# The first input tile's products with the high part of its weights, spread over the transposition stage

## The chip, the cores and the metric

The kernel runs on one core of one Trainium2 chip. The metric is the device time of one execution in microseconds. The engines are named PE (TensorE), ACT (ScalarE), DVE (VectorE), POOL (GpSimd) and SP (SyncE, which only starts DMAs here).

## The reference

One encoder block on 272 tokens (16 meta tokens and 256 of `x`) of width 2048, followed by an expert FFN. The change touches only the first norm and the first 128 columns of the projection behind it:

```python
def rms_norm(x, g):
    xf = x.astype(jnp.float32)
    y = xf * lax.rsqrt(jnp.mean(xf * xf, axis=-1, keepdims=True) + NORM_EPS)
    return (y * g.astype(jnp.float32)).astype(x.dtype)
...
    meta = jnp.broadcast_to(meta_tokens.astype(x.dtype)[None], (bsz, N_META, D_MODEL))
    hs = jnp.concatenate([meta, x], axis=1)
...
        h = rms_norm(hs, norm_mix[l])
        z = h @ w_in[l]
        u_ssm, q, k, v, gates = jnp.split(z, splits, axis=-1)
        y_a = s5_mixer(u_ssm, ssm_lam_re[l], ssm_lam_im[l], ssm_log_dt[l], ssm_b_re[l], ssm_b_im[l],
                       ssm_c_re[l], ssm_c_im[l], ssm_d[l], ssm_w_glu[l], ssm_b_glu[l])
...
        merged = g[:, :, 0] * (y_a @ w_proj_ssm[l]) + g[:, :, 1] * (y_b @ w_proj_attn[l])
        hs = hs + merged @ w_out[l]
        hs = hs + peer_ffn(rms_norm(hs, norm_ffn[l]), peer_w_q[l], peer_k1[l], peer_k2[l],
                           peer_u[l], peer_v[l])
```

## The kernel before

Each engine has its own program in program order; semaphores tie them. A counter such as `s_wdone` (tiles that PE has finished), `s_high` and `s_low` (high and low parts of weight tiles that are ready), `s_hT` and `s_hL` (blocks of the normed input that are ready) is waited on by value. Several counters are raised ahead of time so that the first buffers are free at once: `s_hT` and `s_hL` by 4, `s_uk` by 2.

**Transposition stage.** The rows of `xs` are the tokens, already divided by their root mean square. PE needs them with the 2048 channels on partitions, so for each of KT = 16 blocks of 128 channels it makes three transpositions into bank k % 4 of PSUM: one of the 16 meta tokens (L1372) and two of 128 tokens (L1374). ACT takes the bank, scales it by the norm's weight and rounds it to the high part `hH[k]` (L514); DVE takes the same bank once more and stores what the rounding left, `hL[k]` (L924). A step k of PE waits until `hH[k-4]` and `hL[k-4]` are there, that is, until its bank is free.

**Weight tiles.** A tile of weights, 128 x 2048, comes by DMA into one of the four slots of `ring`, from SP (L366). Its slot is free when PE has finished the tile four before it. ACT rounds it to the high part (`high`, L492), and DVE subtracts to get the low part (`low`, L826). For tile 0 POOL does the subtraction (L419), since DVE is busy with the norm. ACT's high part of tile 0 stands ahead of its sixteen `hH`; that of tile 1 stands right behind them, and DVE's low part of tile 1 right behind the sixteen `hL`. Both queues are strict.

**Column tiles.** For m = 0 to 9 (W_V = 10) PE makes `split_product` into bank m % 2: for each block k the high weights with `hH[k]` (L1359), the same weights with `hL[k]` (L1360) and the low weights with `hH[k]` (L1361), 48 products of 272 columns. Tile 0 waits for the last `hL` and for POOL's low part (`s_first`); each later tile waits for its own low part (`s_low`) and for a bank that ACT has read (`s_uk`). ACT reads a finished tile (L534) behind the high part of the tile two further on, which the same finished tile releases. POOL, meanwhile, copies `hH` and `hL` once the last `hL` is there (L424, L425).

Beside the column tiles DVE works on the coefficients of the state-space part between its low parts. Behind them come value tiles (the first use of banks 2 to 4 after the transpositions), queries and attention, the scan with the gate products, the projections and the expert FFN.

Of the kernel before, what the change touches and what calls it, by code (L numbers as in the profile page):

```python
# [20 lines left out]
ACT = mybir.ActivationFunctionType  # L21
AX_X = mybir.AxisListType.X

P = 128
D = 2048
KT = D // P
META, SEQ = 16, 256
L = META + SEQ
# [18 lines left out]
W_UK, W_V, W_Q, W_GATE, W_GLU, W_PROJ, W_OUT, W_PQ, W_END = 0, 10, 12, 20, 52, 56, 72, 88, 104  # L47
# [11 lines left out]
H2 = L // 2  # L59
# [7 lines left out]
def build(nc, W, keys, par, bw, cw, meta, x, gffn, gfin, u_tab, v_tab, out):  # L67
    top = ExitStack()
    with top:
        def sem(name):  # L70
            return top.enter_context(nc.semaphore(name))

        def sbt(stack, name, shape, dt=F32):
            return stack.enter_context(nc.sbuf_tensor(name, shape, dt))
# [28 lines left out]
        hH = sbt(mix, "hH", [P, KT, L], F32R)  # L103
        yaL, = over(("yaL", [P, CT, SEQ]))
        ukT = sbt(mix, "ukT", [P, 10, L])
# [21 lines left out]
        hL = sbt(pre, "hL", [P, KT, L], F32R)  # L127
# [76 lines left out]
        ps = top.enter_context(nc.psum_tensor("ps", [P, 8, 512], F32))  # L204
# [13 lines left out]
        def wlow(n, m, c):  # L218

            return low_ring[:, n % RING, :].rearrange("p (m c) -> p m c", m=m, c=c)  # L220

        def high_slot(n):

            return (wh1 if n < W_GATE else wh2 if n < W_OUT or n % 4 < 2 else wh3)[:, n % 2, :]

        def whigh(n, m, c):
            return high_slot(n).rearrange("p (m c) -> p m c", m=m, c=c)
# [9 lines left out]
        def nth_low(n):  # L237
            return n - 1 if n < W_Q else W_Q - 1 + n - W_PROJ
# [7 lines left out]
        s_wdone = sem("s_wdone")  # L246
        s_high, s_low = sem("s_high"), sem("s_low")
        s_first = sem("s_first")
# [5 lines left out]
        s_hT, s_hL = sem("s_hT"), sem("s_hL")  # L254
# [52 lines left out]
        s_fsq, s_frt, s_fin, s_out = (sem(n) for n in ("s_fsq", "s_frt", "s_fin", "s_out"))  # L307

        LAG = 2
        FIRST_HALVES = ((), ((2, 0), (2, 1)), ((3, 0),), ((3, 1),), ((4, 0),), ((4, 1),), ((5, 0),), ((5, 1),))  # L310
        FIRST_MINUS = (((2, 0), (2, 1)), ((3, 0), (3, 1)), ((4, 0),), ((4, 1),), ((5, 0),), ((5, 1),), (), ((6, 0), (6, 1)))
        FIRST_OUT = ((0,), (1,), (2,), (), (3,), (), (4,), ())
# [8 lines left out]
        def behind(b, t, k):  # L321

            return (b, t - k) if t >= k else (b - 1, t - k + PPL)
# [152 lines left out]
        def _(act):  # L476
# [10 lines left out]
            def high(n, i=0, back=2):  # L487

                act.wait_ge(s_w[n % RING], 16 * (nth_load(n) + 1) + 16 * i)
                if back:  # L490
                    act.wait_ge(s_wdone, RING + n - back + 1 + RING * i)
                nc.scalar.activation(high_slot(n), ring[:, n % RING, :], ACT.Copy).then_inc(s_high, 1)  # L492
# [29 lines left out]
            for m in range(W_V):  # L522
                act.wait_ge(s_wdone, RING + m + 1)
                high(m + 2)
                if m == SINES:

                    act.wait_ge(s_f0, 1)
                    nc.scalar.activation(disc[:, 6, :], disc[:, 4, :], ACT.Sin, scale=TWO_PI).then_inc(s_trig0, 1)
                    nc.scalar.activation(disc[:, 7, :], disc[:, 4, :], ACT.Sin, scale=TWO_PI / 2).then_inc(s_trig0, 1)
                if m < CT:  # L530
                    for j in range(4):
                        for q in range(2):
                            at = 64 * (j % 2) + 32 * q
                            ins = nc.scalar.activation(ukT[at:at + 32, m, H2 * (j // 2):H2 * (j // 2 + 1)], ps[32 * j:32 * j + 32, m % 2, q:L:2], ACT.Copy)  # L534
                else:
                    ins = nc.scalar.activation(ukT[:, m, :], ps[:, m % 2, 0:L], ACT.Copy)
                ins.then_inc(s_uk, 1)
# [69 lines left out]
            def minus_high(b, t, half):  # L607
                use, q = gate_half(b, t, half)
                act.wait_ge(s_gc[q], 16 * use + 16)
                nc.scalar.activation(gate_lo(q), gate_hi(q), ACT.Copy, scale=-1.0).then_inc(s_gn, 1)  # L610

            def take_y(b, cc):

                ct = 2 * b + cc
                act.wait_ge(s_y, PPC * ct + PPC + PPL)
                for j in range(4):
                    for q in range(2):
                        at = 64 * (j % 2) + 32 * q
                        ins = nc.scalar.activation(flat(yT[32 * j:32 * j + 32, bass.ds(ct, 1), q::2]),
                                                   ps[at:at + 32, 6 + cc, KEPT * (j // 2) + q:KEPT * (j // 2) + q + SEQ // 2], ACT.Copy)  # L620
                ins.then_inc(s_ye, 1)
# [12 lines left out]
            def gate(b, t):  # L634

                g = SPC * b + t
                act.wait_ge(s_wdone, RING + W_GATE + 1 + g)
                nc.scalar.activation(flat(gates_v[:, bass.ds(g, 1), :]), ps[:, t % 2, 0:SEQ], ACT.Identity,  # L638
                                     bias=prm[:, bass.ds(COLS["bgate"][0] + g, 1)]).then_inc(s_gs, 1)

            def scan_body(b, first=False, last=False):
                for t in range(PPL):
# [17 lines left out]
                    else:  # L660
                        gate(*behind(b, t, LAG + 1))
                    if t == PPL - 1:
# [10 lines left out]
            minus_high(*behind(BODIES, 0, 1), 1)  # L673
            gate(*behind(BODIES, 0, LAG + 1))
            act.wait_ge(s_ye, 2 + CT - 1)
            nc.scalar.activation(yT[:, 0:CT - 1, :], yT[:, 0:CT - 1, :], ACT.Gelu_apprx_tanh).then_inc(s_gel, 1)
            gate(*behind(BODIES, 1, LAG + 1))
            take_y(BODIES - 1, 1)
            act.wait_ge(s_ye, 2 + CT)
            nc.scalar.activation(yT[:, CT - 1, :], yT[:, CT - 1, :], ACT.Gelu_apprx_tanh).then_inc(s_gel, 1)  # L680
            gate(*behind(BODIES, LAG, LAG + 1))
            nc.scalar.activation(ybH[:, :, :], ybT[:, :, :], ACT.Copy).then_inc(s_ybh, 1)
# [651 lines left out]
        def _(pe):  # L1334
# [20 lines left out]
            def split_product(dst, n0, xh, xl, ks=range(KT), block0=0, last=KT - 1):  # L1355

                wh, wl = whigh(n0, KT, P), wlow(n0, KT, P)
                for k in ks:
                    nc.tensor.matmul(dst, wh[:, block0 + k, :], xh(k), start=(k == 0), stop=False)  # L1359
                    nc.tensor.matmul(dst, wh[:, block0 + k, :], xl(k), start=False, stop=False)  # L1360
                    ins = nc.tensor.matmul(dst, wl[:, block0 + k, :], xh(k), start=False, stop=(k == last))  # L1361
                return ins


            pe.wait_ge(s_par, 16)
            pe.wait_ge(s_xs, TT)
            pe.wait_ge(s_xsm, 1)
            for k in range(KT):
# [4 lines left out]
                for t in range(TT):  # L1373
                    ins = nc.tensor.transpose(ps[:, k % 4, META + t * P:META + (t + 1) * P], xs[:, t, c], ident)  # L1374
                ins.then_inc(s_tr, 1)
            pe.wait_ge(s_hL, 4 + KT)

            for m in range(W_V):
                if m == 0:
                    pe.wait_ge(s_first, 1)  # L1380
                else:
                    pe.wait_ge(s_low, nth_low(m) + 1)
                pe.wait_ge(s_uk, m + 1)
                split_product(ps[:, m % 2, 0:L], m, lambda k: hH[:, k, :], lambda k: hL[:, k, :]).then_inc(s_wdone, 1)

            for k in range(KT):
# [4 lines left out]
                for t in range(TT + 1):  # L1391
# [5 lines left out]
                    ins = nc.tensor.matmul(dst, hH[:, k, c], wl, start=False, stop=(k == KT - 1))  # L1397
# [60 lines left out]
            def half_gate(b, t, half):  # L1458
                use, q = gate_half(b, t, half)
                if half == 0:  # L1460
                    pe.wait_ge(s_gs, SPC * b + t + 1)
                half_tile(t, half, HEADS // RING + SPC // RING * b + t // RING, q, use)
# [112 lines left out]
            def scan_body(b, first=False, last=False):  # L1575
                for t in range(PPL):
                    cc = t // PPC
                    if first:
                        for g, half in FIRST_HALVES[t][0:1]:
                            half_gate(b, g, half)  # L1580
                    else:
                        half_gate(*behind(b, t, LAG), 0)
                    if t % PPC == 3:
# [11 lines left out]
                    if first:  # L1595
                        for g, half in FIRST_HALVES[t][1:]:
                            half_gate(b, g, half)
                    else:
                        half_gate(*behind(b, t, LAG), 1)

# [46 lines left out]
            for c in range(4):  # L1647
                pe.wait_ge(s_hs, 2 * c + 2)
                for g in range(4):
# [5 lines left out]
                    for k in range(4 * g, 4 * g + 4):  # L1655
                        for T in range(TT):
# [3 lines left out]
                            ins = nc.tensor.matmul(dst, mH[:, k, rows], wl[:, k % 4, :], start=False, stop=(k == KT - 1))  # L1660
# [35 lines left out]
            for T in range(TT):  # L1696
                tokens = slice(T * P, (T + 1) * P)
                for q in range(2):
                    weights_in(W_PQ + q)
                    w = wtile(W_PQ + q, KT, P)  # L1700
                    for k in range(KT):
                        if T == 0 and q == 0 and k == KT - 4:
                            pe.wait_ge(s_h2T, 4 + KT)
                        ins = nc.tensor.matmul(ps[:, 4 + q, tokens], w[:, k, :], h2T[:, k, tokens], start=(k == 0), stop=(k == KT - 1))
                    ins.then_inc(*((s_fp, 1) if T == 0 else (s_wdone, 1)))
                pe.wait_ge(s_key, 16)
                for half in range(2):
                    pe.wait_ge(*((s_fq, half + 1) if T == 0 else (s_qp, 3 + half)))
                    ins = nc.tensor.matmul(ps[:, 6, (2 * T + half) * NK:(2 * T + half + 1) * NK], qp[:, half, tokens],
                                           keyt[:, 0, half, :], start=True, stop=True)  # L1710
# [112 lines left out]
```

## Time and profile before

| what | us |
|---|---|
| median of 3 runs | 2058.37 |
| lowest, highest | 2055.93, 2059.32 |
| the profiled execution | 2053.23 |
| its span, first to last instruction | 2051.4 |
| PE busy in it | 1748.9 |

The span is the time from the first to the last instruction of the profiled execution; its device time is 1.8 us longer. All times of the trace are counted from the span's start. A timeline row has the start, the busy time, the engine, the line, the operation, output and inputs, their shapes, the number of instructions merged in the row, and in brackets the idle time ahead of it and who ended it. A PE row's busy time reaches to the end of its pipeline, so the distance between the starts of two rows, not their busy time, is what a product costs in a dense row of them.

### The profile page before, as it was taken

How to read it: one execution, taken by the hardware profiler on the slowest of the kernel's cores; microseconds unless marked ns; L12 is line 12 of the kernel's file. 1: busy time of each engine (PE TensorE's matmuls, PEld its weight loads, DVE VectorE, ACT ScalarE, POOL GpSimd, SP SyncE). 2: the span in 40 equal slices, each digit the busy share in tenths (PEclk: the TensorE clock that was granted, in tenths of full speed). 3: DMA queues.
4: the chain of work that ended last, by engine and by line, in shares of the span. 5: the costliest groups of instructions: out<-in, count | busy, mean ns of one | idle time of the engine just before them, and what ended most of it. 6: DMA issues, size and time to landing. Idle time of an engine off the chain costs nothing.

```text
span 2051.4 us, 23984 instructions
## 1 busy us (share of the span) xinstructions
PE 1748.9 (85%) x7792; PEld 1091.3 (53%) x7792; DVE 1286.3 (63%) x2444; ACT 475.7 (23%) x1056; POOL 805.0 (39%) x711
## 2 busy tenths in 40 slices
PE   6999899999999999789879977777777777778776
PEld 5988788888998855335425522233232222223222
DVE  4635888885454455665667667667666665666654
ACT  6533555655343201101011001002000000000001
POOL 2022233330540053454445554444554554554431
PEclk9999999999999999999999999999999999999999
DMA  4578789987455699999999999999999999999997
GB/s 186 164 173 184 173 193 209 213 193 237 168 187 182 223 394 421 421 421 422 422 422 422 418 422 421 421 422 413 421 418 411 422 417 389 422 404 412 422 422 298
DMA packets 115890, 687.60 MB, mean 335 GB/s; under 512 B 12880, under 2 KB 12880, under 8 KB 41168
## 3 DMA queue, kind: packets, MB, share of 16 engines
q0 software_dynamic: 96768, 589.34, 75.7%
q1 hardware_dynamic: 19040, 97.24, 13.4%
q8 instruction: 42, 0.69, 0.1%
q14 instruction: 40, 0.33, 0.0%
HBM read 684.44 MB, written 2.10 MB: 335 GB/s over the span
## 4 chain that ended last, share of the span: by engine, by line
PE 46%; DMA 35%; issue 7%; DVE 6%; POOL 4%; ACT 1%; DVEq 0%; POOLq 0%; SPq 0%; ACTq 0%
DMA uv<-u_tab,eid 31%; PE ps L1726 14%; PE ps L1442 4%; PE ps L1676 3%; PE ps L1359 2%; PE ps L1360 2%; PE ps L1361 2%; POOL uv L472 2%; DMA parts<-W 2%; PE ps L1447 2%; DVE uv L1295 2%; PE ps L1449 2%; PE ps L1448 2%; PE ps L1659 1%; PE ps L1658 1%
## 5 line engine op out<-in xcount | busy, mean ns | idle before, releaser
L1726 PE MATMUL ps<-uv,dg 128*128 128x512 f32 x2048 | 959.6, 615 | 265.6 <-DVE dg L1301 256.6
L1295 DVE CUSTOM_DVE_ANT_0 uv<-uv,xn 128x2048 f32<-128x2048 f32 x256 | 586.9, 2293 | 377.4 <-DMA uv<-u_tab,eid 359.1
L1726 PEld LDWEIGHTS ps<-uv,dg 128*128 128x128 f32 x2048 | 381.1, 194 | 821.7 <-issue 458.8
L472 POOL DMA_INDIRECT uv<-v_tab,eid x256 | 274.9, 1074 | 590.9 <-PE ps L1726 360.4
L469 POOL DMA_INDIRECT uv<-u_tab,eid x256 | 353.0, 1379 | 199.5 <-issue 184.9
L772 ACT ACTIVATE ga<-av 128x1 f32<-128x1 f32 x256 | 51.9, 203 | 1185.1 <-DVE av L1295 1185.1
L826 DVE TENSOR_TENSOR low_ring<-ring,wh 128x2048 fp32r<-128x2048 f32 x43 | 101.0, 2352 | 76.6 <-ACT wh L492 76.6
L1301 DVE TENSOR_SCALAR dg<-prm,ga,gw 128x128 f32<-128x128 f32 x256 | 95.0, 371 | 66.8 <-ACT ga L772 32.6
L1447 PE MATMUL ps<-hH,parts 128*128 128x256 f32 x400 | 123.8, 310 | 2.4 <-DMA parts<-W 2.3
L442 POOL DMA_DIRECT2D parts<-W x80 | 70.4, 880 | 139.3 <-ACT parts L610 111.7
L438 POOL DMA_DIRECT2D parts<-W x80 | 47.1, 588 | 179.6 <-PE ps L1449 111.9
L1449 PE MATMUL ps<-hH,parts 128*128 128x256 f32 x400 | 112.2, 280 | 0.0
L1448 PE MATMUL ps<-hLx,parts 128*128 128x256 f32 x400 | 112.2, 280 | 0.0
L1442 PE MATMUL ps<-xn,ring 128*128 128x256 f32 x480 | 111.6, 382 | 0.1
L492 ACT ACTIVATE wh<-ring 128x2048 fp32r<-128x2048 f32 x44 | 84.3, 1917 | 114.7 <-PE ps L1361 82.1
L1676 PE MATMUL ps<-h2T,ring 128*128 128x256 f32 x448 | 100.8, 379 | 0.0
L1676 PEld LDWEIGHTS ps<-h2T,ring 128*128 128x128 f32 x448 | 85.0, 190 | 21.8 <-issue 11.5
L1442 PEld LDWEIGHTS ps<-xn,ring 128*128 128x128 f32 x480 | 88.3, 190 | 12.7 <-ACT gates L638 0.7
L1447 PEld LDWEIGHTS ps<-hH,parts 128*128 128x128 f32 x400 | 75.3, 188 | 8.7 <-issue 4.7
L1448 PEld LDWEIGHTS ps<-hLx,parts 128*128 128x128 f32 x400 | 75.6, 189 | 1.0
L1449 PEld LDWEIGHTS ps<-hH,parts 128*128 128x128 f32 x400 | 75.4, 188 | 0.0
L610 ACT ACTIVATE parts<-parts 128x640 fp32r<-128x640 f32 x60 | 44.0, 734 | 94.5 <-DMA parts<-W 94.5
(284 smaller groups left out, 2238.3 us busy)
## 6 DMA issues: line engine op xcount, KB each, us to landing
ring<-W SPq DMA_DIRECT2D x64, 1024.0 KB, 4.8
parts<-W POOLq DMA_DIRECT2D x160, 320.0 KB, 5.4
ring<-W SPq DMA_DIRECT2D x40, 384.0 KB, 5.2
xn<-x SPq DMA_DIRECT2D x4, 1024.0 KB, 8.2
uv<-u_tab,eid POOLq DMA_INDIRECT x256, 15.5
uv<-v_tab,eid POOLq DMA_INDIRECT x256, 14.2
bwt<-bw SPq DMA_DIRECT2D x8, 256.0 KB, 6.0
cwt<-cw SPq DMA_DIRECT2D x8, 256.0 KB, 6.1
```

Source lines behind the costliest of these rows:

```text
L469: pool.indirect_dma_start(uv[:, s, 0, :], None, u_tab, at).then_inc(s_u[s], 16)
L472: pool.indirect_dma_start(uv[:, s, 1, :], None, v_tab, at).then_inc(s_vv[s], 16)
L492: nc.scalar.activation(high_slot(n), ring[:, n % RING, :], ACT.Copy).then_inc(s_high, 1)
L826: nc.vector.tensor_tensor(low_ring[:, n % RING, :], ring[:, n % RING, :], high_slot(n), ALU.subtract).then_inc(s_low, 1)
L1295: nc.vector.tensor_tensor_reduce(uv[:, j % UV, 0, :], uv[:, j % UV, 0, :], xn[:, T, :], 1.0, 0.0, ALU.mult, ALU.add, av[:, hh, j:j + 1]).t ...
L1301: nc.vector.tensor_scalar(dg[:, j % 2, :], ident, ga[:, hh, j:j + 1], gw[:, hh, j:j + 1], ALU.mult, ALU.mult).then_inc(s_dg, 1)
L1442: nc.tensor.matmul(dst, whole(t)[:, k, :], hX[:, k, :], start=(k == 0), stop=False)
L1447: nc.tensor.matmul(dst, wh[:, m, :], hH[:, k, META:L], start=False, stop=False)
L1448: nc.tensor.matmul(dst, wh[:, m, :], hLx[:, k, :], start=False, stop=False)
L1449: ins = nc.tensor.matmul(dst, wl[:, m, :], hH[:, k, META:L], start=False, stop=(k == 2 * PART - 1))
L1676: ins = nc.tensor.matmul(ps[:, 4 + q % 2, 0:SEQ], w[:, k, :], h2T[:, k, :], start=(k == 0), stop=(k == KT - 1))
L1726: ins = nc.tensor.matmul(ps[:, 4 * T + n, :], dg[:, j % 2, :], uv[:, j % UV, 1, n * 512:(n + 1) * 512], start=False, stop=last and i == 2 ...
```

## The change

The column tile 0 is taken out of the loop over tiles. It gets bank 4 (`FIRST_BANK`) in place of bank 0, which the transpositions use. From step k = 4 on, PE makes two products of tile 0, high weights with `hH[k-4]` and with `hL[k-4]`, behind the transpositions of step k. The pairs 12 to 15 come after the last transpositions, each behind a wait for its `hL`. Then come the 16 products with the low weights, now in one row, and `s_wdone` is raised as before. ACT reads tile 0 from bank 4. Nothing changes on the queues of DVE, POOL and SP.

```diff
+        FIRST_BANK = 4
...
-                            ins = nc.scalar.activation(ukT[at:at + 32, m, H2 * (j // 2):H2 * (j // 2 + 1)], ps[32 * j:32 * j + 32, m % 2, q:L:2], ACT.Copy)
+                            ins = nc.scalar.activation(ukT[at:at + 32, m, H2 * (j // 2):H2 * (j // 2 + 1)], ps[32 * j:32 * j + 32, m % 2 if m else FIRST_BANK, q:L:2], ACT.Copy)
...
             pe.wait_ge(s_par, 16)
+            wh0, wl0 = whigh(0, KT, P), wlow(0, KT, P)
+            first_out = ps[:, FIRST_BANK, 0:L]
+
+            def high_terms(k):
+                nc.tensor.matmul(first_out, wh0[:, k, :], hH[:, k, :], start=(k == 0), stop=False)
+                nc.tensor.matmul(first_out, wh0[:, k, :], hL[:, k, :], start=False, stop=False)
+
             pe.wait_ge(s_xs, TT)
             pe.wait_ge(s_xsm, 1)
             for k in range(KT):
...
                 ins.then_inc(s_tr, 1)
-            pe.wait_ge(s_hL, 4 + KT)
-
-            for m in range(W_V):
-                if m == 0:
-                    pe.wait_ge(s_first, 1)
-                else:
-                    pe.wait_ge(s_low, nth_low(m) + 1)
+                if k >= 4:
+                    pe.wait_ge(s_high, 1)
+                    high_terms(k - 4)
+            for k in range(KT - 4, KT):
+                pe.wait_ge(s_hL, 4 + k + 1)
+                high_terms(k)
+            pe.wait_ge(s_first, 1)
+            for k in range(KT):
+                ins = nc.tensor.matmul(first_out, wl0[:, k, :], hH[:, k, :], start=False, stop=(k == KT - 1))
+            ins.then_inc(s_wdone, 1)
+
+            for m in range(1, W_V):
+                pe.wait_ge(s_low, nth_low(m) + 1)
                 pe.wait_ge(s_uk, m + 1)
                 split_product(ps[:, m % 2, 0:L], m, lambda k: hH[:, k, :], lambda k: hL[:, k, :]).then_inc(s_wdone, 1)
```

PE's instructions at the steps 3 to 5 of the transposition stage, before (`prm` holds the identity matrix, `gates` is the memory of `xs`):

```order
7 L1372 MATMUL ps<-prm,gates 128x16
8 L1374 MATMUL ps<-prm,gates 128x128 x2
9 L1372 MATMUL ps<-prm,gates 128x16
10 L1374 MATMUL ps<-prm,gates 128x128 x2
11 L1372 MATMUL ps<-prm,gates 128x16
12 L1374 MATMUL ps<-prm,gates 128x128 x2
```

The same place of PE's queue in the changed kernel, where L1380 and L1382 are the transpositions and L1371 and L1372 the pair of `high_terms`:

```order
7 L1380 MATMUL ps<-prm,gates 128x16
8 L1382 MATMUL ps<-prm,gates 128x128 x2
9 L1380 MATMUL ps<-prm,gates 128x16
10 L1382 MATMUL ps<-prm,gates 128x128 x2
11 L1371 MATMUL ps<-hH,wh 128x272
12 L1372 MATMUL ps<-hL,wh 128x272
13 L1380 MATMUL ps<-prm,gates 128x16
14 L1382 MATMUL ps<-prm,gates 128x128 x2
15 L1371 MATMUL ps<-hH,wh 128x272
16 L1372 MATMUL ps<-hL,wh 128x272
```

Two products of tile 0 now stand between the transpositions of one step and those of the next, from step 4 on.

PE's instructions from the last transpositions into tile 0, before:

```order
31 L1372 MATMUL ps<-prm,gates 128x16
32 L1374 MATMUL ps<-prm,gates 128x128 x2
33 L1359 MATMUL ps<-hH,wh 128x272
34 L1360 MATMUL ps<-hL,wh 128x272
35 L1361 MATMUL ps<-hH,low_ring 128x272
36 L1359 MATMUL ps<-hH,wh 128x272
```

And in the changed kernel, from the last transpositions to the first products of tile 1 (L1360 to L1362 are `split_product` there):

```order
53 L1380 MATMUL ps<-prm,gates 128x16
54 L1382 MATMUL ps<-prm,gates 128x128 x2
55 L1371 MATMUL ps<-hH,wh 128x272
56 L1372 MATMUL ps<-hL,wh 128x272
57 L1371 MATMUL ps<-hH,wh 128x272
58 L1372 MATMUL ps<-hL,wh 128x272
...
63 L1371 MATMUL ps<-hH,wh 128x272
64 L1372 MATMUL ps<-hL,wh 128x272
65 L1392 MATMUL ps<-hH,low_ring 128x272 x16
66 L1360 MATMUL ps<-hH,wh 128x272
```

Between the last transpositions and tile 1 there are five pairs and the sixteen low-part products, 26 products in place of 48.

## Rows read from the trace of the kernel before

**Rows 1.** Busy time of each engine by stretches of 10 us, columns named.

```profile
core 0: us, PE busy (x) PEld busy (x) DVE busy (x) ACT busy (x) POOL busy (x), PEclk, DMA share, GB/s
20.00:30.00 10.00, 8.89 (x33) 5.26 (x32) 5.50 (x11) 6.54 (x12) 1.32 (x2) 1.00 0.00 0
40.00:50.00 10.00, 10.00 (x83) 10.00 (x82) 5.88 (x14) 5.91 (x14) 0.00 (x0) 1.00 0.47 160
```

**Rows 2.** Timeline of the transposition stage; last row: L1374 alone, duration ns min/median/max, starts.

```profile
13.79 1.89 ACT L492 ACTIVATE wh<-ring 128x2048 fp32r<-128x2048 f32 x1
...
14.45 0.26 PE L1372 MATMUL ps<-prm,gates 16*128 16x16 f32 x1 [14.45 <-DVE gates L919]
...
15.25 0.28 PE L1372 MATMUL ps<-prm,gates 16*128 16x16 f32 x1
...
26.09 0.28 PE L1372 MATMUL ps<-prm,gates 16*128 16x16 f32 x1
...
26.30 0.69 PE L1374 MATMUL ps<-prm,gates 128*128 128x128 f32 x2
...
26.92 0.28 PE L1372 MATMUL ps<-prm,gates 16*128 16x16 f32 x1
27.03 0.49 ACT L514 ACTIVATE hH<-ps,prm 128x272 fp32r<-128x272 f32 x1 [0.35 <-PE ps L1374]
...
27.55 0.50 DVE L924 SCALAR_TENSOR_TENSOR hL<-ps,prm,hH 128x272 fp32r<-128x272 f32 x1 [0.34 <-ACT hH L514]
...
L1374 PE MATMUL ps<-prm,gates x32: 420/448/476, 14.6 to 27.4; 128*128 128x128 f32 x32
```

**Rows 3.** Timeline, from the last hH to the middle of tile 0.

```profile
27.86 0.49 ACT L514 ACTIVATE hH<-ps,prm 128x272 fp32r<-128x272 f32 x1 [0.35 <-PE ps L1374]
28.24 1.90 ACT L492 ACTIVATE wh<-ring 128x2048 fp32r<-128x2048 f32 x1
...
28.93 0.59 PE L1359 MATMUL ps<-hH,wh 128*128 128x272 f32 x1 [1.11 <-DVE hL L924]
28.96 3.49 POOL L424 TENSOR_TENSOR xn<-hH,hL 128x1536 f32<-128x1536 f32 x1 [8.68 <-DVE hL L924]
...
29.33 0.43 PE L1360 MATMUL ps<-hL,wh 128*128 128x272 f32 x1
...
30.18 4.42 DVE L826 TENSOR_TENSOR low_ring<-ring,wh 128x2048 fp32r<-128x2048 f32 x1 [1.30 <-ACT wh L492]
...
32.27 0.41 PE L1361 MATMUL ps<-hH,low_ring 128*128 128x272 f32 x1
...
32.50 0.31 PE L1359 MATMUL ps<-hH,wh 128*128 128x272 f32 x1
```

**Rows 4.** Timeline of PE, SP and DVE where tile 1 follows tile 0.

```profile
36.51 0.28 PE L1361 MATMUL ps<-hH,low_ring 128*128 128x272 f32 x1
36.63 0.29 PE L1359 MATMUL ps<-hH,wh 128*128 128x272 f32 x1
...
36.97 6.30 SPq L366 DMA_DIRECT2D ring<-W  x2
...
38.87 2.29 DVE L826 TENSOR_TENSOR low_ring<-ring,wh 128x2048 fp32r<-128x2048 f32 x1 [4.27 <-ACT wh L492]
```

**Rows 5.** Timeline of PE, then stretches (columns as rows 1), scan stage.

```profile
218.72 0.39 PE L1447 MATMUL ps<-hH,parts 128*128 128x256 f32 x1 [2.31 <-DMA parts<-W]
...
251.76 1.97 PE L1484 MATMUL ps<-prm,hs 128*128 128x128 f32 x8
...
220.30:223.60 3.30, 3.30 (x50) 2.89 (x49) 3.30 (x9) 0.00 (x0) 1.43 (x2) 0.50 0.70 147
251.00:254.30 3.30, 3.30 (x24) 2.85 (x23) 3.22 (x10) 0.00 (x0) 0.00 (x0) 0.50 1.05 264
254.40:257.80 3.40, 3.40 (x23) 2.92 (x20) 3.21 (x9) 3.38 (x9) 0.87 (x1) 1.00 0.69 174
```

**Rows 6.** Waits from 0 to 130 us: who waited for whom, total, times, longest.

```profile
POOL parts L438 <- PE ps L1361: 54.9, 1, 54.9
```

## The prediction

> **What bounds the kernel now.** The change touches only the first 40 us, so I read that stretch. The view by stretches first: from 40 us on PE is busy 10.00 us of 10 while the ten column tiles of the first projection run, but from 20 to 30 us only 8.89 [rows 1]. So whatever moves the start of the first PE-bound tile moves everything behind it, and the question is what sets that start.
>
> The timeline of one step of the transposition stage comes next [rows 2]. Step k is one 16-column product at L1372 and two 128-column ones at L1374, then ACT's hH[k], then DVE's hL[k]. The L1372 rows stand at 26.09 and 26.92, a pitch of 0.83 us, and sixteen steps fill 14.45 to 27.8, when the last hH starts [rows 3]. Is it PE or ACT that sets this pitch? ACT works 0.49 us of each 0.83 and is idle for 0.34 of it, released by PE L1374; DVE works 0.50 and waits for ACT. Nobody is full but PE, whose matmul rows leave no hole. Nor can it be ACT's release that paces PE: a step waits for step k-4 alone, done over two microseconds earlier, and steps 0 and 1, which wait for no hH at all, already stand 0.80 us apart (14.45 and 15.25) [rows 2]. **The transposition stage is PE-bound**, and this is what the change loads further.
>
> Then the end of the stage [rows 3]. The last hH runs at 27.86, ACT makes the high part of tile 1 at 28.24 (1.90 us), DVE its low part at 30.18 for 4.42 us, ready at 34.60. PE starts tile 0 at 28.93 after 1.11 us of idleness. Its products stand 0.226 us apart up to 32.27 (272 columns in 0.226 us is the 1.2 GHz level) and 0.125 us apart from 32.50 on (33 of them up to 36.63), the 2.4 GHz level. (The granted-clock column reads 1.00 before that, because its record starts there; the spacing of the rows is what I go by.) Tile 1 starts at 36.63, straight behind tile 0 [rows 4]. So there are two chains to tile 1: PE's own, which ends at 36.6, and hH[15] - high(1) - low(1), which ends at 34.6. The second has only 2.0 us of slack.
>
> **The change, part by part.** Nothing is computed less: 32 of tile 0's 48 products go elsewhere. 22 of them (11 pairs, after the steps 4 to 14) now stand ahead of the transpositions of step 15, one more pair behind step 15, four pairs behind that, then 16 low-part products.
>
> What it can gain: PE's idle 1.11 us, and less behind the stage. But even with PE's chain at nothing, tile 1 can't start before 34.60, its low part's end. The gain is capped at 36.63 - 34.60 = 2.0 us, 0.1% of the span.
>
> What it costs: each pair at the 1.2 GHz pace is 2 x 0.226 = 0.45 us in the middle of a stage that PE bounds. From below, a pair could take 0.32 us, if it also fills the 0.13 us by which the last product of a step is longer than such a transposition back to back. That last one: the two L1374 end at 26.30 + 0.69 = 26.99, one alone takes 0.42, so the second began at 26.57, 0.35 us ahead of the next L1372 [rows 2]. Back to back it is (1.97 - 0.42) / 7 = 0.22 us: eight L1484 took 1.97 at the low level [rows 5]. From above 0.62 us: the first product behind the stage took 0.40 us to the next (28.93 to 29.33 [rows 3]) and one more at 0.226. I take 0.45, since satisfied waits cost nothing at a tile change (36.51 to 36.63 is the plain spacing [rows 4]), and the added waits on s_high are satisfied from 15.7 on (13.79 + 1.89 us, ACT's first high part [rows 2]). That delays hH[15] by 11 x 0.45 = 5.0 us (3.5 to 6.8), and with it, on unchanged ACT and DVE queues, high(1) and low(1). Low(1) takes 4.42 us where the next one takes 2.29 [rows 3, 4]; what differs is POOL's copying beside it (L424 from 28.96, L425 behind it). That waits for the last hL, so it moves along and low(1) stays long. Ready: 34.60 + 5.0 = 39.6.
>
> PE's chain meanwhile: step 15's transpositions end at about 32.8, high pair 11 at 33.2, pairs 12 to 14 by 34.6, pair 15 by 35.0 (its hL is ready just ahead of 28.93 + 5.0 = 33.9). The 16 low-part products end between 37.0 (16 x 0.125) and 38.6 (16 x 0.226). At either clock **PE then waits 1.0 to 2.6 us for low(1)**, and tile 1 starts at about 39.65 instead of 36.63: **+3.0 us**, with the bounds of the pair +1.5 to +4.8.
>
> Edits costed at nothing, and their cover: the other bank (ACT's eight reads of tile 0 are the same reads from another bank, and bank 4 is next written by the value tiles, eight tiles later); the load of tile 4, which waits for tile 0's end, 36.97 before [rows 4] and at most 38.6 now, 6.3 us for two, wanted only four tiles on, at some 6.0 us each (11 us of cover or more); high(2), released by tile 0's end as well, wanted when tile 1 ends, six us later. Does a later stage take the 3 us back? DVE's low parts are released by ACT's high parts and those by PE's tile counter; POOL's weight streams wait 54.9 us for that counter [rows 6]. Each is released by PE's progress, so all shift together, and I carry the whole +3.0 us to the end.
>
> **What the clock may do.** The rows show two things that disagree. The transposition stage ran from 14.45 to 27.8 us, and the products behind it still started at the low level's spacing [rows 2, 3]. But later, from 251.0 to 254.3, at granted clock 0.50, PE ran eight transpositions L1484 without a gap, with a few products ahead of them and behind, and went up straight after (0.50, then 1.00) [rows 5]. The difference that I see is density: eight transpositions in 1.97 us there, three in 0.83 us with pauses here.
>
> The Trainium skill ("TensorE: Matmul & The Clock Gate", Part 4: PE-mode transpose) says that the full clock doesn't engage for transposes, since they don't count as busy time in the same way. By that rule only the pairs would count in the new mixture, and the sum stands as it is; the stage before agrees with it, the rows from 251 us on are hard to square with it. Were transpositions to count in full, the sum would be that of rival 1.
>
> **The rivals.** Rival 1, the clock rises within the mixed stretch. For it: the rows at 251 us, and a denser PE. Against: 13.4 us of transpositions that didn't do it; pairs are only 0.45 of 1.28 us. Price: if it rises at about 23 us, four pairs have cost 1.8 us, and each remaining step of 0.83 shrinks to some 0.55 (an estimate: its products at half the time, its pauses unchanged) while its pair costs 0.25, so these break even. hH[15] is some 1.6 us late, low(1) ready at 36.2: tile 1 at 36.3, -0.4 us. The earliest rise gives the cap, -2.0. So 2058.0, still no measurable change.
>
> Rival 2, on the other side: **the new hole drops the clock or keeps it low, and tile 1 starts at 1.2 GHz.** Before, PE ran without a hole from 28.93, and was at the high level 3.6 us later. Now 1.0 to 2.6 us of idleness stand ahead of tile 1. An idle 2.31 us before 218.72 was followed by granted clock 0.50 at 220.3 [rows 5]. 3.6 us at the low level do the work of 2.0, so 1.6 us more: +4.6 us, 2063.0. It decides where the hole is 2 us or so, or where the clock hasn't risen by 39.6.
>
> Rival 3, the loss is hidden: some later wait (the DMA waits at 113 to 220 us) isn't released by PE and absorbs the 3 us: 2058.4. Against: the release chain told above.
>
> **How the numbers follow.** The profiled execution spans 2051.4 us and took 2053.2; the median of the runs is 2058.4 (2055.9 to 2059.3). I add to the median: 2058.4 + 3.0 = **2061.4 us**. Chances: forecast 0.45, rival 2 0.25, rival 1 0.20, rival 3 0.10. Range: down to 2057.0, which takes in most of rival 1 and 3; up to 2064.6, which takes in rival 2 and the forecast with a pair at 0.62 us (+4.8). A measurement of this kernel can tell about 0.2%, 4.1 us, from no change. Slower by more than that: three quarters of rival 2, and the upper fifth of the forecast: 0.28. Faster by that is beyond the cap of 2.0 us, and only scatter gives it: 0.03. Within 0.2%: 0.69.
>
> **What the new profile would show.** Pitch of L1380 (the old L1372): 0.83 for the first four steps, then 1.28. Last hH at 32.8 instead of 27.86; DVE's low part of tile 1 from 35.2 to 39.6, and PE idle before tile 1, released by DVE low_ring. If the pitch falls to 0.8 or less in the middle, rival 1 holds; if the first products of tile 1 stand 0.226 us apart, rival 2. A pair that costs much less than 0.45 us, or a tile 1 that doesn't wait for its low part, would break the sum. If tile 1 starts near 39.6 but the span is as before, it is rival 3.

## The result, and the profile after

| | us, median | lowest to highest | runs |
|---|---|---|---|
| before | 2055.61 | 2052.48 to 2061.20 | 22 |
| after | 2059.86 | 2054.51 to 2063.12 | 22 |

The ratio is 1.0016, with a 95% interval of 1.0011 to 1.0022: the changed kernel takes 3.3 us more (2.3 to 4.5). The two medians alone lie 4.25 us apart. The loss is real, and by the ratio it is within the 0.2% (4.1 us) that the prediction set as the bound of "no change"; by the medians it lies just at that bound. The forecast was +3.0 us.

In the timeline of the changed kernel the stage reads as it was worked out. One step with a pair, rows of PE, ACT and DVE (columns as in rows 2):

```profile
20.28 0.57 PE L1371 MATMUL ps<-hH,wh 128*128 128x272 f32 x1
20.65 0.43 PE L1372 MATMUL ps<-hL,wh 128*128 128x272 f32 x1
20.66 0.49 ACT L515 ACTIVATE hH<-ps,prm 128x272 fp32r<-128x272 f32 x1 [0.80 <-PE ps L1382]
21.01 0.28 PE L1380 MATMUL ps<-prm,gates 16*128 16x16 f32 x1
21.18 0.50 DVE L925 SCALAR_TENSOR_TENSOR hL<-ps,prm,hH 128x272 fp32r<-128x272 f32 x1 [0.79 <-ACT hH L515]
21.23 0.69 PE L1382 MATMUL ps<-prm,gates 128*128 128x128 f32 x2
...
22.30 0.28 PE L1380 MATMUL ps<-prm,gates 16*128 16x16 f32 x1
```

The starts of L1380 are 1.29 us apart, where [rows 2] had 0.83 between the same instructions, then L1372: a pair costs 0.45 us. ACT's idle time ahead of each hH has grown from 0.35 to 0.80 us, by that same 0.45: PE still paces the stage, and ACT waits for it longer. PE is busy for 10.00 us of the stretch from 20 to 30 us, which was 8.89 in [rows 1]. The busier PE has gained nothing.

The end of the stage and the start of tile 1, the rows that answer to [rows 3, 4]:

```profile
32.24 0.49 ACT L515 ACTIVATE hH<-ps,prm 128x272 fp32r<-128x272 f32 x1 [0.80 <-PE ps L1382]
32.63 1.91 ACT L493 ACTIVATE wh<-ring 128x2048 fp32r<-128x2048 f32 x1
...
33.35 3.49 POOL L425 TENSOR_TENSOR xn<-hH,hL 128x1536 f32<-128x1536 f32 x1 [13.66 <-DVE hL L925]
...
34.27 2.55 PE L1392 MATMUL ps<-hH,low_ring 128*128 128x272 f32 x16
34.57 8.75 DVE L827 TENSOR_TENSOR low_ring<-ring,wh 128x2048 fp32r<-128x2048 f32 x2 [1.30 <-ACT wh L493]
...
39.04 0.39 PE L1360 MATMUL ps<-hH,wh 128*128 128x272 f32 x1 [2.22 <-DVE low_ring L827]
39.27 0.29 PE L1361 MATMUL ps<-hL,wh 128*128 128x272 f32 x1
39.40 0.29 PE L1362 MATMUL ps<-hH,low_ring 128*128 128x272 f32 x1
```

The last hH starts at 32.24 instead of 27.86, the low part of tile 1 at 34.57 instead of 30.18 (the row merges two low parts; the first ends at 39.0), and PE, which in the kernel before went on to tile 1 at 36.63 without a wait, is idle for 2.22 us until DVE's low part is there. Tile 1 starts at 39.04. This execution's stage began 0.6 us earlier (13.85, against 14.45 in [rows 2]), so from the first transposition tile 1 is 3.0 us later (25.19 against 22.18). The products of tile 1 stand 0.12 us apart: it runs at the 2.4 GHz level from the start.

The spans of the two profiled executions differ by more, 2060.1 against 2051.4 us. That isn't the change: the profiled execution of before, 2053.23 us, lies near the low end of that kernel's range, that of after, 2061.96, near the high end of its own. Of the 8.7 us only 3.1 lie between the first transposition and tile 2.

For the experiments I read one number of each trace besides the runs: from the first transposition to the first product of tile 2, by which the start of the kernel and the clock's later dips drop out. It is 28.16 us before and 31.27 after.

### The profile page after: what moved, and what is told of

Same layout as the page of the kernel before. It is cut to its first block, busy times and chain, and to the rows that moved or that the text cites. A ratio compares the mean times of both kernels' runs of the same rounds, so it can differ in the third digit from the quotient of the medians.

```text
span 2060.1 us, 23983 instructions
## 1 busy us (share of the span) xinstructions
PE 1756.0 (85%) x7792; PEld 1096.2 (53%) x7792; DVE 1287.8 (63%) x2444; ACT 476.1 (23%) x1056; POOL 795.7 (39%) x711
## 4 chain that ended last, share of the span: by engine, by line
PE 44%; DMA 35%; issue 8%; DVE 7%; POOL 4%; ACT 1%; DVEq 0%; POOLq 0%; ACTq 0%; SPq 0%
DMA uv<-u_tab,eid 31%; PE ps L1740 13%; PE ps L1456 4%; DMA parts<-W 3%; POOL uv L473 3%; PE ps L1690 3%; PE ps L1360 2%; PE ps L1361 2%; PE ps L1362 2%; DVE uv L1296 2%; PE ps L1461 2%; PE ps L1463 2%; PE ps L1462 2%; PE ps L1673 1%; PE ps L1672 1%
## 5 line engine op out<-in xcount | busy, mean ns | idle before, releaser
L470 POOL DMA_INDIRECT uv<-u_tab,eid x256 | 340.5, 1330 | 199.5 <-issue 184.0
```

Of the source, the lines that this page charges most:

```text
L470: pool.indirect_dma_start(uv[:, s, 0, :], None, u_tab, at).then_inc(s_u[s], 16)
```

## Experiments

Each was run in five rounds beside the kernel before. Ratios and gains in us are against that kernel, with 95% intervals in brackets.

**Pairs behind the stage.** From the changed kernel:

```diff
-                if k >= 4:
-                    pe.wait_ge(s_high, 1)
-                    high_terms(k - 4)
-            for k in range(KT - 4, KT):
+            pe.wait_ge(s_high, 1)
+            for k in range(KT):
                 pe.wait_ge(s_hL, 4 + k + 1)
                 high_terms(k)
```

> Bank 4 and the order pairs first, low products last are kept, but all 16 pairs stand behind the transpositions of step 15; nothing is interleaved. Theory (the loss is the pairs inside the PE-bound stage, which delay hH[15] and so the low part of tile 1): step pitch stays 0.83 us, hH[15] and the low part of tile 1 stand as in the kernel before, and PE only gains its 1.1 us of idleness ahead of tile 0: tile 1 starts 1 to 1.5 us earlier relative to the first transposition (34.6 is the floor), so -1 to -1.5 us. Rival (the loss comes from the other bank, or from the order of the 48 products with the low ones last): still +3 us.

Ratio 0.9987 (0.9978 to 0.9996), -2.7 us (-4.5 to -0.8). First transposition to tile 2: 26.86 us, 1.3 less than before. Timeline of PE and ACT at the end of the stage:

```profile
26.79 0.28 PE L1380 MATMUL ps<-prm,gates 16*128 16x16 f32 x1
26.90 0.49 ACT L515 ACTIVATE hH<-ps,prm 128x272 fp32r<-128x272 f32 x1 [0.35 <-PE ps L1382]
...
27.01 0.69 PE L1382 MATMUL ps<-prm,gates 128*128 128x128 f32 x2
...
27.35 0.57 PE L1371 MATMUL ps<-hH,wh 128*128 128x272 f32 x1
```

The products follow the last transposition without the 1.11 us of waiting in [rows 3], and ACT's 0.35 us is back. So neither the bank nor the order of the 48 products costs anything; what costs is where the eleven pairs stand. The forecast of -1 to -1.5 us lies within the interval, and the trace gives -1.3. The version is faster than both kernels; against the one before it is 0.13%.

**Six pairs in the stage instead of twelve** (five ahead of step 15):

```diff
-                if k >= 4:
+                if k >= 10:
                     pe.wait_ge(s_high, 1)
-                    high_terms(k - 4)
-            for k in range(KT - 4, KT):
+                    high_terms(k - 10)
+            for k in range(KT - 10, KT):
```

> Pairs only behind the steps 10 to 15, five of them ahead of the transpositions of step 15 instead of eleven; the other ten pairs behind the stage. Theory: hH[15] later by 5 x 0.45 = 2.3 us instead of 5.0; the low part of tile 1 is ready at 36.9 where it was 34.6, so tile 1 starts 0.3 us later than before: +0.3 us, no measurable change, and PE waits for the low part only some tenths of a us. Rival (any interleaving costs the same, by a switch of mode between transpositions and products): near +3 us.

Ratio 1.0000 (0.9991 to 1.0009); 28.77 us to tile 2, 0.6 more than before. The size is as forecast (+0.3 us, no measurable change), and a fixed cost of any interleaving, +3 us, is ruled out. But the trace got there by another way. Timeline of PE:

```profile
23.51 0.28 PE L1380 MATMUL ps<-prm,gates 16*128 16x16 f32 x1
...
24.80 0.28 PE L1380 MATMUL ps<-prm,gates 16*128 16x16 f32 x1
...
26.06 0.23 PE L1380 MATMUL ps<-prm,gates 16*128 16x16 f32 x1
...
26.84 0.23 PE L1380 MATMUL ps<-prm,gates 16*128 16x16 f32 x1
...
35.08 0.39 PE L1360 MATMUL ps<-hH,wh 128*128 128x272 f32 x1 [2.10 <-DVE low_ring L827]
...
36.58 0.43 PE L1361 MATMUL ps<-hL,wh 128*128 128x272 f32 x1
36.80 0.43 PE L1362 MATMUL ps<-hH,low_ring 128*128 128x272 f32 x1
```

Two full steps take 1.29 us; from 26.0 on they take 0.78: the clock rose in the mixed stage, which is rival 1. Tile 0 was finished early, PE stood idle for 2.10 us, and within tile 1 the spacing goes to 0.22 us: the clock fell, which is rival 2. The stretches show the granted clock (columns as rows 1):

```profile
36.30:39.60 3.30, 3.30 (x17) 3.30 (x16) 3.27 (x3) 0.85 (x4) 0.91 (x1) 0.50 0.28 117
39.70:42.60 2.90, 2.90 (x26) 2.90 (x25) 0.90 (x4) 0.00 (x0) 0.00 (x0) 1.00 0.00 0
```

Tile 1 took 7.61 us (35.08 to 42.69) where it takes 5.98 in [rows 4]'s kernel: 1.6 us, the price that the prediction gave for this.

**The second chain cut.** The high part of tile 1 is made behind hH[5], its low part on POOL behind that of tile 0; DVE's own `low(1)` goes, and PE waits for `s_first` at 2 ahead of tile 1:

```diff
                 nc.scalar.activation(hH[:, k, :], ps[:, k % 4, 0:L], ACT.Copy, scale=col("gmix", k, k + 1)).then_inc(s_hT, 1)
-            high(1)
+                if k == 5:
+                    high(1)
...
             pool.tensor_tensor(low_ring[:, 0, :], ring[:, 0, :], high_slot(0), ALU.subtract).then_inc(s_first, 1)
+            pool.wait_ge(s_high, 2)
+            pool.tensor_tensor(low_ring[:, 1, :], ring[:, 1, :], high_slot(1), ALU.subtract).then_inc(s_first, 1)
```

> The changed kernel with the second chain cut: ACT makes the high part of tile 1 behind hH[5] instead of behind hH[15], and POOL makes its low part behind that of tile 0. Theory: the step pitch stays 1.28 us, but tile 1 starts right behind tile 0, at 36.7 instead of 39.04 on the changed kernel's clock: 2.4 us of the 3 come back, so +0.6 to +0.9 us against the kernel before. Rival (the loss is PE's own work at the low clock, not the wait for the low part): stays at +3.

Ratio 0.9994 (0.9984 to 1.0003), -1.2 us (-3.3 to +0.6); 28.69 us to tile 2, +0.5. The step pitch is still 1.29 us. Timeline of PE, the last of tile 0 and the first of tile 1:

```profile
35.23 1.67 PE L1395 MATMUL ps<-hH,low_ring 128*128 128x272 f32 x12
36.74 0.29 PE L1363 MATMUL ps<-hH,wh 128*128 128x272 f32 x1
```

No bracket: tile 1 follows at once. With the pairs just as they are in the changed kernel, 2.6 of the 3.1 us are gone as soon as tile 1 doesn't hang on hH[15]. That shows the chain hH[15], high(1), low(1) to carry the loss. The forecast for the runs, +0.6 to +0.9 us, lies at or just beyond the upper end of what they gave; the trace's +0.5 is close to it.

**One low product more** in each of the steps 8 to 15 (`low_term(k - 8)` behind `high_terms(k - 4)`, the other eight behind the stage):

```diff
                     high_terms(k - 4)
+                if k >= 8:
+                    pe.wait_ge(s_first, 1)
+                    low_term(k - 8)
```

> The changed kernel with one low product of tile 0 more in each of the steps 8 to 15, so three products beside the transpositions; seven of them ahead of step 15. Theory: hH[15] later by another 7 x 0.226 = 1.6 us, tile 1 too: +4.6 us against the kernel before, step pitch 1.51 us in these steps. Rival 1 of the prediction (a denser PE raises the clock in the mixed stage): the pitch falls below 1.2 us in the last steps and the total is +1 to +3 us.

Ratio 1.0011 (1.0002 to 1.0021), +2.3 us (+0.4 to +4.3). The pitch is 1.51 us for five steps, as forecast, then the clock rises at 30.9 and the last step takes 0.90. So rival 1 came true here, late. It brought nothing: PE waited 4.2 us for the low part of tile 1, the clock was low from 37.8 to 44.5, and the profiled execution has tile 2 at 33.96 us. Timeline of PE at tile 1:

```profile
39.58 0.59 PE L1360 MATMUL ps<-hH,wh 128*128 128x272 f32 x1 [4.20 <-DVE low_ring L827]
```

That is 5.8 us later than in the kernel before, where the runs lose 2.3: this execution took the longest of its eleven (2062.08 us). That the clock went another way in the others is likely, but not shown. The run doesn't tell how the loss grows with the number of products moved, since the clock moved with it.

**POOL's copies later.** The changed kernel, with POOL waiting for DVE's low part of tile 1 before it copies:

```diff
             pool.wait_ge(s_hL, 4 + KT)
+            pool.wait_ge(s_low, 1)
```

> The changed kernel, in which POOL's two copies of hH and hL wait until DVE has made the low part of tile 1. If that low part takes 4.4 us because POOL copies beside it, it takes 2.3 us now and ends at 36.9 instead of 39.0; tile 1 starts there, 0.4 us behind tile 0's end, and 2.1 of the 3 us come back: about +0.9 us against the kernel before. The next low part then runs beside the copies, but has cover. If POOL is not the cause, it stays at 4.4 us and the total at +3.

Ratio 1.0005 (0.9996 to 1.0014), +1.0 us (-0.8 to +2.9); 29.15 us to tile 2, +1.0. Timeline of DVE, then of POOL:

```profile
34.71 2.29 DVE L828 TENSOR_TENSOR low_ring<-ring,wh 128x2048 fp32r<-128x2048 f32 x1 [1.30 <-ACT wh L494]
39.37 3.44 DVE L828 TENSOR_TENSOR low_ring<-ring,wh 128x2048 fp32r<-128x2048 f32 x1 [2.36 <-ACT wh L494]
```

```profile
37.14 3.52 POOL L426 TENSOR_TENSOR xn<-hH,hL 128x1536 f32<-128x1536 f32 x1 [17.30 <-DVE low_ring L828]
40.60 4.39 POOL L427 CAST hLx<-hL 128x2560 fp32r<-128x2560 f32 x1
```

The low part of tile 1 takes 2.29 us instead of 4.42, ends as tile 0 does, and in the trace two thirds of the loss are gone (2.1 of 3.1 us). The next low part now meets POOL's copy and shows how: it starts at 39.37 under L426, which ends at 40.66, and ends at 42.81, 2.15 us after. It looks as if it stood still until POOL was done and then ran at its own pace. [Rows 3] fit the same: L424 ends at 32.45, low(1) at 34.60, 2.15 us after. In the changed kernel the copy ends at 36.84 and low(1) at 38.99, again 2.15 us after. POOL waits in its turn. Timeline of POOL in the version where it makes low(1) itself and DVE's next low part starts only at 38.97:

```profile
36.97 2.34 POOL L428 CAST hLx<-hL 128x2560 fp32r<-128x2560 f32 x1
```

The same cast took 4.40 us in the changed kernel, where DVE's low part ran for its first 2.2 us. The Trainium skill ("SBUF — State Buffer", SBUF: two separate sides) says just this, that VectorE and GpSimd share a pair of ports as an exclusive lock and the later one is blocked for the whole instruction; the 2.15 us, the same each time, agree with it.

**A warm start.** A "warm start" means here that PE reaches the stage at the 2.4 GHz level. To price a pair at that level, PE makes products of a constant tile, whose result nobody reads, while it waits for the norm anyway. The first form, on the kernel before, has 40 of them; each runs as two instructions:

```diff
+            pe.wait_ge(s_warm, 1)
+            for _ in range(40):
+                nc.tensor.matmul(ps[:, 5, 0:256], ucur[:, 0, 0:128], ucur[:, 0, 0:256], start=True, stop=True)
```

> The kernel before with 40 products of 128x256 (a constant tile, result never read) on PE ahead of the transposition stage, where PE waits for the norm anyway; they begin at about 2 us. They take 0.43 us each at the low level and 0.23 at the high one, so the clock rises among them and the stage starts at the high level. If transpositions alone keep the clock up, the step pitch is some 0.55 us throughout, the stage is 3 to 4 us shorter and tile 0 runs at 0.125 us a product: -4 to -6 us. If they don't count, the pitch is short for some steps only, the clock falls within the stage, and the gain is 1 to 2 us at most, with tile 0 as before.

> The changed kernel with the same 40 products ahead. Tells whether the mixed stage can hold the high level where it could not reach it. Theory (the price of a pair is that of the low level): if the clock holds, a pair costs at most 0.25 us, the step pitch is below 0.85 us, and the changed kernel's loss of 3 us is gone: -3 to -6 us against the kernel before, about the same as the kernel before with the warm start. If the clock falls in the stage: pitch 1.28 again after some steps, 0 to +3 us.

> The version with all pairs behind the stage (-2.7 us measured) and the 40 products ahead. If the high level survives the stage or a part of it, this gains what the warm start gains on the kernel before plus up to 1.3 us: -4 to -7 us; if the clock falls within the stage, -2 to -4 us.

Kernel before with it: ratio 1.0014 (1.0005 to 1.0023), +2.9 us. Changed kernel: 1.0024 (1.0015 to 1.0033), +4.9 us. Pairs behind: 1.0009 (1.0000 to 1.0018), +1.9 us. The gains forecast for a clock that holds were 4 to 6, 3 to 6 and 4 to 7 us; in all three traces it held through the stage, and all three forecasts were misses. I had mis-sized the filling, which I took for 40 instructions: it lasts until 21.4 us and delays the stage by 7 us. The inside of the stage still answers the question. Stretches of the kernel before with the warm start, the filling and the stage (columns as rows 1):

```profile
6.40:21.00 14.60, 14.60 (x69) 12.84 (x68) 4.42 (x14) 7.95 (x8) 4.51 (x1) 1.00 0.91 378
21.40:30.00 8.60, 8.56 (x49) 5.36 (x48) 6.98 (x15) 7.32 (x16) 0.00 (x0) 1.00 0.00 0
```

and its timeline of PE, then two steps of the changed kernel with the same start:

```profile
21.41 0.23 PE L1377 MATMUL ps<-prm,gates 16*128 16x16 f32 x1
...
21.94 0.23 PE L1377 MATMUL ps<-prm,gates 16*128 16x16 f32 x1
```

```profile
27.51 0.23 PE L1385 MATMUL ps<-prm,gates 16*128 16x16 f32 x1
...
27.86 0.37 PE L1376 MATMUL ps<-hH,wh 128*128 128x272 f32 x1
28.07 0.29 PE L1377 MATMUL ps<-hL,wh 128*128 128x272 f32 x1
28.29 0.23 PE L1385 MATMUL ps<-prm,gates 16*128 16x16 f32 x1
```

There are sixteen bare steps at 0.53 us, the high level held for 8.6 us of nothing but transpositions; with a pair, a step takes 0.78. So a pair costs 0.45 us at the low level and 0.25 at the high one, and the change loses at either: in the traces it is 4.0 us behind the kernel before with the same start (25.75 against 21.73 us to tile 2). Of these, 2.4 us are tile 1's later start, ahead of which PE waits 3.18 us for the low part, and 1.6 the clock, which falls at 40.6. By the ratios it is 2 us.

**A shorter filling**, 20 in place of 40:

> The kernel before with 20 of the leading products instead of 40 (each runs as two instructions, so 40 of them in place of 80): they end at 12.7 to 13.9 us, before the stage needs PE. The version with 40 had the stage start at 21.4 in place of 14.4 and still lost only 2.9 us; its steps were 0.53 us apart and tile 2 began 21.7 us behind the first transposition, against 28.2. If the start of the stage stays at 14.4: -6.4 us. If the clock falls in the short hole before the stage or in it, -1 to -3 us.

> The changed kernel with 20 leading products. With 40 its steps were 0.78 us apart where they carry a pair and 0.53 where not, so a pair costs 0.25 us at the high level. Eleven pairs delay hH[15] by 2.75 us against the kernel before with the warm start, and the low part of tile 1 is what PE waits for (3.2 us of idleness with 40): tile 1 some 2.5 us later than in e8_warm20_before, and the hole may bring the clock down for tile 1, 1.6 us more: -2 to -4 us against the kernel before. So the change loses at the high level too.

> Pairs behind the stage with 20 leading products: as e8_warm20_before, but PE starts tile 0 1.1 us earlier; tile 1 is then bound by its low part, so 0 to -1 us beyond e8_warm20_before: -6 to -7 us.

> The same with the high part of tile 1 made behind hH[5] and its low part on POOL, so that tile 1 follows tile 0 without a hole: another 0 to 1.3 us, -6.5 to -8.5 us against the kernel before.

| kernel with 20 | ratio, 95% interval | us | first transposition at | to tile 2 |
|---|---|---|---|---|
| before | 0.9993 (0.9985 to 1.0002) | -1.4 | 13.98 | 26.83 |
| after | 1.0009 (1.0000 to 1.0019) | +1.9 | 14.07 | 28.51 |
| pairs behind | 0.9976 (0.9966 to 0.9986) | -4.9 | 14.18 | 21.72 |
| pairs behind, low(1) on POOL | 0.9982 (0.9973 to 0.9990) | -3.7 | 14.02 | 24.61 |

The filling now ends in time, but the high level doesn't always survive the stage: in the kernel before the steps were 0.53 us, then 0.83 from 17 us on. Stretches of it, filling, first steps, the rest:

```profile
6.90:12.90 6.00, 6.00 (x29) 5.13 (x27) 3.44 (x14) 5.07 (x7) 0.00 (x0) 1.00 1.01 421
14.00:17.10 3.10, 2.89 (x17) 1.85 (x18) 1.40 (x4) 2.85 (x6) 1.80 (x1) 1.00 1.02 423
17.20:25.00 7.80, 7.80 (x29) 4.20 (x28) 4.89 (x11) 4.64 (x10) 2.62 (x1) 0.50 0.29 119
```

In the version with the pairs behind it held throughout. The same stretch there:

```profile
14.10:22.80 8.70, 8.42 (x49) 5.46 (x50) 6.60 (x14) 8.03 (x16) 4.53 (x1) 1.00 0.62 256
```

Up to the last transposition PE's program is the same in these two kernels, so the difference in the clock is one between executions and not one of code. With it, tile 1 started at 29.81, and tile 2 stood 6.4 us earlier in its stage than in the kernel before.

The last version is another matter. Timeline of ACT and PE in it, then a stretch:

```profile
17.90 1.90 ACT L497 ACTIVATE wh<-ring 128x2048 fp32r<-128x2048 f32 x1
...
20.86 0.20 PE L1388 MATMUL ps<-prm,gates 16*128 16x16 f32 x1 [1.26 <-DVE hL L930]
...
21.00:25.00 4.00, 4.00 (x16) 2.19 (x15) 2.70 (x7) 2.26 (x5) 3.40 (x1) 0.50 0.01 4
```

ACT's high part of tile 1 stands here ahead of hH[6]. At steps of 0.53 us four banks don't cover its 1.90 us: PE is idle for 1.26 us ahead of step 10, and the rest of the stage runs at the low level. At the pitch of 1.29 us the same move of high(1) cost PE nothing. Whether this hole brought the clock down isn't shown, as it fell without one in the kernel before.

Of the four forecasts two were plain misses. The changed kernel was to gain 2 to 4 us and lost 1.9; in its trace the clock fell early in the stage, and once more behind a hole of 3.20 us. The last version was to gain 6.5 to 8.5 us and gained 3.7 (2.1 to 5.5). The kernel before was to gain 6.4 us, or 1 to 3 if the clock falls: it fell in the trace, and the runs gave 1.4. The pairs behind were to gain 6 to 7 us and gained 4.9 (2.9 to 7.0). The order of the four is the one expected but for the last two, which the runs don't tell apart (0.9976 and 0.9982, with overlapping intervals). What this group settles: with a warm start, too, the change is behind the kernel before, by 3.3 us of the ratios and 1.7 in the traces, and the pairs behind the stage ahead of both. The lowest median of the study is that with pairs behind and 20 leading products, 2050.4 us against 2056.3.

## Why the prediction was right

**What bounds the stage.** Right. The prediction held PE to pace it, against the profile's note that PE's loads wait for ACT. Timeline of the kernel before:

```profile
25.05 0.50 DVE L924 SCALAR_TENSOR_TENSOR hL<-ps,prm,hH 128x272 fp32r<-128x272 f32 x1 [0.33 <-ACT hH L514]
...
26.92 0.18 PEld L1372 LDWEIGHTS ps<-prm,gates 16*128 16x128 f32 x1 [0.33 <-ACT hH L514]
```

The pitch grew by exactly the pair's length in the changed kernel and ACT's idle time with it. One reading on the way was wrong: the step that a PE step waits for was not done "over two microseconds earlier". The last step waits for hL[11], the DVE row shown, which ends at 25.55, 1.4 us ahead. At the pitches of these two kernels that is cover enough, so nothing in the sum hung on it. At 0.53 us a step it ran out, as the last version above shows.

**The price of a pair.** 0.45 us, the value taken, neither 0.32 nor 0.62: measured 1.287 - 0.834 = 0.453.

**The second chain.** Right, and the step that made the result: 2.0 us of slack, 5.0 us of delay, 3.0 us left. Cutting that chain (POOL makes the low part) brought back 2.6 of the 3.1 us in the trace, taking the pairs out of the stage brought back all of it and 1.3 more, and both with the rest of the change in place.

**Low(1) stays long.** Right. It took 4.42 us again, and 2.29 when POOL's copies waited.

**PE's idle time ahead of tile 1.** Forecast as 1.0 to 2.6 us, measured as 2.22, towards the end where the clock has risen among the low products (at 35.1).

**Nothing takes the loss back.** Right: +3.3 us by the ratio of the runs, +3.1 in the trace at tile 2. Rival 3 is out.

**How close the numbers came.** With the two stages laid on the same start, the trace has the last hH at 32.84, the low part of tile 1 from 35.17 to 39.59 and tile 1 at 39.64, where the prediction had 32.8, 35.2 to 39.6 and 39.65. For the total some of the closeness is luck. The forecast of 2061.4 us was built on a median of three runs, 2058.37, and 22 runs of the same kernel gave 2055.61. So the measured 2059.86 lies 1.5 us below the forecast although the rise was, if anything, larger than the 3.0 us forecast.

**The clock.** In the profiled execution neither rival occurred: no rise in the mixed stage in eleven steps, and no fall in the hole. But both mechanisms were then seen in a close relative, the version with six pairs, in one and the same execution, at the prices given (steps of 0.78 us, tile 1 longer by 1.6 us). With 20 leading products the changed kernel, too, had its clock rise within the mixed stage, at 22.7 us. So it was right to give them a chance; whether 0.20 and 0.25 were the right sizes isn't shown. What the single profile of the changed kernel can't tell is how many of its 22 runs, which spread over 8.6 us, had one or the other. That stays open. It also stays open what decides it, since the same mixture of instructions raised the clock in one execution after three steps and not in another after eleven.

**The rule on transpositions.** The prediction weighed the rule of the Trainium skill ("TensorE: Matmul & The Clock Gate", Part 4: PE-mode transpose) that the full clock doesn't engage for transposes against the rows from 251 us on. The runs with a warm start settle half of it: transpositions alone held the high level, granted clock 1.00, for 8.6 us, so the rule doesn't hold here for keeping the level. In no bare stage seen here did they bring it up from the low one, which agrees with the rule. Where the filling ended 0.8 us ahead of the stage the level was lost after some steps in one kernel and kept in another.

## What to carry to other kernels

Filling an engine's time helps only where that engine isn't the one that paces the stage: here PE looked partly idle, but each step waited for PE, so all work put between its steps moved everything that hangs on the last step. Before moving work forward, find every chain that ends at the next stage's start and its slack; the one that is not critical now (here by 2.0 us) is what the work moved will run into. The same products right behind the last step cost nothing and gained the wait that was there.

## What the runs showed of the hardware

- A low part on DVE that starts under a POOL copy ended 2.15 us after the copy's end each time (in the kernel before, in the changed one and in the one with POOL's copies later), and took 4.42 or 3.44 us instead of 2.29: it waits rather than slows. POOL's cast took 4.40 us where DVE's low part was under way and 2.34 where not.
- Transpositions alone kept PE's high clock for 8.6 us (steps of 0.53 us instead of 0.83). In another execution with the same transpositions it was lost after 3 us, and the same sixteen steps never reached it from the low level.
- Five profiled executions had PE idle for over 2 us ahead of tile 1. In four the low level followed: six pairs (2.10 us; tile 1 took 7.61 us), changed kernel with 40 leading products (3.18; 7.63) and with 20 (3.20; 7.63), one low product more (4.20; 8.33). In the changed kernel itself 2.22 us of idleness were followed by none (tile 1 took 6.08).
